# Attention step of a two-layer hybrid block: the scores' second part ahead of the transposes on TensorE, the scaling and the output copy ahead of the transposes' rounding on ScalarE

## The reference, cut to what matters

```
s = einsum('bqhgd,bkhd->bhgqk', q, k) * scale      # fp32 scores
p = softmax(s)                                     # swa: masked, with a sink
o = einsum('bhgqk,bkhd->bqhgd', p, v)
y = sigmoid(g_m)*((o_m*silu(z_m)) @ w_o_mla) + ... # also swa and ax
x = x + gate * (y @ w_out)
```

## Time and profile before

| what | value |
|---|---|
| median of 3 runs | 1756.91 us |
| the profiled execution's own time | 1756.88 us |
| its span | 1755.1 us |
| TensorE busy | 1679.7 us |
| ScalarE busy | 1049.0 us |
| VectorE busy | 1037.7 us |
| GpSimd busy | 625.0 us |
| mean granted TensorE clock | 0.987 of full speed |

### The profile page before, as it was taken

The page is one execution under the profiler, slowest core; times in us unless marked ns, Lnnn a source line. Parts: engine busy times, 40 slices in busy tenths (PEclk is TensorE's granted clock), DMA queues, the critical chain, the costliest instruction groups (busy, mean ns, idle before and its releaser), DMA issues.

```text
span 1755.1 us, 26992 instructions
## 1 busy us (share of the span) xinstructions
PE 1679.7 (96%) x10400; PEld 1471.6 (84%) x10400; DVE 1037.7 (59%) x2164; ACT 1049.0 (60%) x1919; POOL 625.0 (36%) x426
## 2 busy tenths in 40 slices
PE   7899999999999999999999999999999998999997
PEld 3778888889888899999889996788888887888787
DVE  6445766665566655545774556566676666555633
ACT  3435777776667767765221254678777678777322
POOL 2433333333333332323322344344344433333442
PEclk9999999999999999999999999999999999999999
DMA  9111111111121112012635222111122221212642
GB/s 332 40 37 29 26 46 37 49 31 49 49 55 49 42 31 55 26 48 57 219 117 197 90 87 61 41 38 46 51 53 67 72 73 32 69 52 53 204 148 93
DMA packets 178531, 129.51 MB, mean 74 GB/s; under 512 B 21658, under 2 KB 167652, under 8 KB 178404
## 3 DMA queue, kind: packets, MB, share of 16 engines
q1 hardware_dynamic: 174240, 115.36, 23.0%
q10 hardware_dynamic: 2884, 8.24, 1.3%
q0 software_dynamic: 1280, 4.20, 0.7%
HBM read 123.58 MB, written 4.19 MB: 73 GB/s over the span
## 4 chain that ended last, share of the span: by engine, by line
PE 77%; DVE 11%; ACT 8%; issue 3%; DMA 1%; POOL 1%; SPq 0%; DVEq 0%; ACTq 0%
PE acc L1393 56%; PE wide L1444 6%; PE ptp L1462 6%; PE pv L1475 4%; PE pv L1476 3%; DVE nmax L2051 2%; ACT e L1710 2%; DVE pt L2076 1%; ACT w_hi L1627 1%; DVE k_m L1579 1%; DVE q_s L1579 1%; ACT k_m L1570 1%; DVE k_s L1579 1%; DMA w_raw<-in_ada_w 1%; ACT e L1717 0%
## 5 line engine op out<-in xcount | busy, mean ns | idle before, releaser
L1834 POOL TENSOR_TENSOR w_lo<-w_raw,w_hi 128x1024 fp32r<-128x1024 f32 (+2 forms) x192 | 390.9, 2039 | 566.4 <-ACT w_hi L1627 565.0
L1393 PE MATMUL acc<-h_hi,w_hi 128*128 128x512 f32 (+2 forms) x1320 | 466.1, 354 | 13.0 <-DVE lf L1954 5.1
L1393 PE MATMUL acc<-h_hi,w_lo 128*128 128x512 f32 (+2 forms) x1320 | 462.4, 351 | 0.0
L1393 PE MATMUL acc<-h_lo,w_hi 128*128 128x512 f32 (+2 forms) x1320 | 458.6, 351 | 0.5 <-POOL h_lo L1896 0.5
L1393 PEld LDWEIGHTS acc<-h_hi,w_hi 128*128 128x128 f32 (+1 forms) x1320 | 249.5, 189 | 52.0 <-issue 12.4
L1725 ACT ACTIVATE pt<-ptp 128x512 fp32r<-128x512 f32 (+3 forms) x312 | 165.9, 563 | 198.2 <-PE ptp L1462 196.4
L1393 PEld LDWEIGHTS acc<-h_hi,w_lo 128*128 128x128 f32 (+1 forms) x1320 | 249.8, 189 | 34.0
L1393 PEld LDWEIGHTS acc<-h_lo,w_hi 128*128 128x128 f32 (+1 forms) x1320 | 246.9, 189 | 34.8 <-POOL h_lo L1896 0.9
L2051 DVE TENSOR_REDUCE nmax<-wide 128x1 f32<-128x768 f32 (+3 forms) x240 | 190.0, 792 | 112.1 <-PE wide L1444 108.6
L1888 POOL TENSOR_TENSOR o_t<-o_half,o_t 64x256 f32<-64x256 f32 x120 | 91.9, 766 | 436.9 <-DVE o_half L2083 434.8
L1717 ACT ACTIVATE e<-e,einv 128x768 f32<-128x768 f32 (+3 forms) x240 | 193.4, 806 | 57.2 <-DVE einv L2068 56.8
(11 more groups left out here) (215 smaller groups left out, 3065.8 us busy)
## 6 DMA issues: line engine op xcount, KB each, us to landing
w_raw<-in_w_in SPq DMA_DIRECT2D x102, 512.0 KB, 3.9
w_raw<-in_ada_w SPq DMA_DIRECT2D x48, 512.0 KB, 5.3
w_raw<-in_w_out SPq DMA_DIRECT2D x16, 512.0 KB, 3.5
w_raw<-in_w_in SPq DMA_DIRECT2D x16, 256.0 KB, 3.2
w_raw<-in_w_o_mla SPq DMA_DIRECT2D x16, 256.0 KB, 2.7
w_raw<-in_w_o_swa SPq DMA_DIRECT2D x16, 256.0 KB, 2.7
w_raw<-in_w_o_ax SPq DMA_DIRECT2D x16, 256.0 KB, 2.8
w_raw<-in_mla_w_uq SPq DMA_DIRECT2D x16, 144.0 KB, 2.3
```

Source lines behind the costliest of these rows:

```text
L1393: ins = nc.tensor.matmul(dst, lhs, rhs, start=first, stop=last)
L1834: nc.gpsimd.tensor_tensor(w_lo[s][:, 0:k], w_raw[s][:, 0:k], f(w_hi[s][:, 0:k]), ALU.subtract).then_inc(w_lo_ready, 1)
```

## The change

Inside each step of the loop, the transposes' event `T` moves from behind `PV` to behind `SB`, `N` and `OC`, and `OC` moves from behind `X` to ahead of `T`.

```diff
             valued, waiting = waiting[:2], waiting[2:]
-            for t in valued:
-                T(t)
             if u:
                 SB(u)
             if 0 < i <= len(units):
                 emit("N", u=units[i - 1])
+            if turned:
+                emit("OC", pa=turned)
+            for t in valued:
+                T(t)
             if u:
                 X(u)
-            if turned:
-                emit("OC", pa=turned)
             for t in valued:
                 emit("TL", t=t)
```

## The result

The changed kernel takes **1786.86 us** (median of 4 runs, 1786.74 to 1788.28) against 1755.95 us for the kernel before in the same session. The ratio is 1.0177, 95% interval 1.0165 to 1.0189: slower by 30.9 us. The forecast was 1775 us, range 1749 to 1791. The profiled execution has a span of 1785.1 us, 30.0 more than before.

A forecast was written before the change was run, and what follows sets the result against it. TensorE, busy 96% of the span, was taken as the bound. Terms 12.0 − 1.2 + 3.2 + 5.0 + 2 + 3 − 6 gave +18 us on 1756.88 us: 1775 us, range 1749 to 1791.

The forecast's parts named there:

- What bounds it: Whole kernel: TensorE, busy 96%; inside the attention its values' matmuls wait 31 times, scores 3 times, 32.3 us in all.
- The late step, +1.0 us: Step at 1244 us, reciprocal late: roundings follow scaling and copy, the chain ends 1.0 us later, all of it lost.
- The early step, −0.4 us: Step at 650 us, reciprocal early: scaling fills idle time, chain 0.4 us shorter, exponential 0.7 us earlier, worth nothing there.
- The values' waits: Values' matmuls: output's sum late +12.0, early −1.2; low part +3.2; new waits for steps not yet stalling +5.0 us.
- Lost cover at scores, +2: TensorE's scores lose the transposes' cover while waiting for the exponential: some four places at 0.5 us, +2 us.
- The clock, +3: TensorE's clock falls to 1.2 GHz behind long waits: two more such waits, about 1.5 us lost each, +3 us.
- Catching up, −6: A longer TensorE stall lets the other engines catch up, and earlier exponentials bring the reciprocal forward: −6 us.
- the bounds of the unknown terms: Cover (0 to +5), new waits (0 to +15) and catching up (−15 to 0) were said to span 1757 to 1794 us.
- Rival A: The shorter chain wins: most stalls of the values' matmuls have an early reciprocal and shrink, 1749 us; chance 0.20.
- The rule on the queues: ScalarE's and VectorE's queues are strictly first in, first out: a waiting scaling holds the roundings; otherwise near 1750 us.
- B: The two cancel: stalls grow at late steps, vanish at early ones, and projections absorb the rest, 1757 us; chance 0.15.
- C: The delay feeds itself: each late exponential makes the next reciprocal late, 56 steps at +0.7, 1796 us; chance 0.10.

The follow-up runs named there:

- run 1: Only TensorE's half of the change, scores ahead of transposes, ScalarE's order as before, against the kernel before: 1764.37 us, ratio 1.0050.
- runs 5 and 6: Scaling by a column of ones, without the wait for the reciprocal: 5 on the changed kernel, 1749.04 us; 6 on the kernel before, 1752.99 us.
- Run 9: The changed kernel with VectorE's reciprocal moved from the next step's start to its own step's end: 1742.41 us, ratio 0.9921 against the kernel before.
- ScalarE's half alone: Kernel before with only ScalarE's scaling and output copy moved ahead of the rounding, TensorE keeping transposes ahead of scores: 1795.79 us, ratio 1.0226.
- runs 8, 10 and 11: Against the kernel before: 8, scaling behind copy and exponential, 1821.44 us; 10 and 11, reciprocal and scaling at own step's end, scores or transposes first, 1809.55, 1819.19 us.

## Why the prediction was right, point by point

- **What bounds it.** Right in the main. The loss appears in the attention, as waits of the values' matmuls (+19.0 us), of scores (+2.3) and as clock (+10.0); the rest of the kernel did not get longer.
- **The late step, +1.0 us.** The chain measured 3.94 us against 2.92: +1.02. But "all of it is lost" did not hold: TensorE's step grew by 0.74 us. **The early step, −0.4 us**, and the exponential 0.7 earlier: measured −0.43 and 0.79.
- **The values' waits.** My terms for them (12.0 − 1.2 + 3.2 + 5.0) were +19.0 net, and the matmuls' rows grew by 19.0. That the two agree to the tenth is luck. The split was off: waits for the output's sum grew by 17.0, with 14 new ones, and for the low part by 2.0; I had 10.8 and 3.2, and 5 for new ones of either kind. The rows do not say how much an old wait grew by.
- **Lost cover at scores, +2.** Measured +2.3 at matmuls; without the late scaling it is larger, 8.2 us of waits in run 1.
- **The clock, +3: too small.** I had two more falls, and there were four more, one of ten microseconds: +10.0 us in the attention. The mean clock of the whole trace, 0.987 to 0.985, hides this, as outside the attention less clock was missing (−6.7 us).
- **Catching up, −6: too large.** The late step shows that it exists, 0.27 us there. But the attention's waits grew by the full 20.9 us, what the terms without it add up to (19.0 and 2), so nothing of it is left over in the total.
- **The size.** +18 was forecast and about +31 measured. By the terms, the missing parts are the clock (7), catching up (6) and some 3 to 4 us of waits that the matmuls' rows do not show; the time outside the attention, which was 4.9 us shorter in the profiled execution, takes from these. The measured time lies nearer to the upper end of the range than to 1775.
- **Two slips in the working.** "Six take 0.7 at 1244": the row of six holds three matmuls of 256 columns and three of 512, and they took 1.14 us. The 0.24 us for two was right all the same (670.75 to 670.99 in the changed kernel). And the bounds of the unknown terms give 1759 to 1794, not 1757.
- **A number I did not foresee.** Rival A was to decide at fewer than some 25 waits for the reciprocal. There are 165. I had counted only the 56 in which ScalarE came to the scaling ahead of the reciprocal in the order of before; with the scaling first it does so in 109 more. Most of these waits replace waits for transposes: the two together grew by only 18.6 us.
- **The rule on the queues.** That ScalarE keeps strict order (the Trainium skill, "TensorE: Matmul & The Clock Gate", section "Architectural detail: the array is 16× 32×32, not 1× 128×128") agrees with runs 5 and 6: taking away one wait of a later operand, with all work left in place, gave back 37.8 us.
- **The rivals.** A does not happen here. Run 9, with the reciprocal early, comes nearest to it: 48 waits for the reciprocal, 20.4 us of waits of the values' matmuls and not 31.2, and 1742.41 us. B did not come. C, the delay that feeds itself, did not come at 1796 either, but ScalarE's half alone reached 1795.8.

## What to carry to other kernels

Before an operation that waits for another engine's tiny result is put ahead of one whose operand is ready, look where the tiny result stands in *its* engine's queue, however much idle time there seems to be. Here the 0.16 us reciprocal behind up to 2.8 us of key splits decided between −0.8% and +1.8% for the same order on ScalarE. When a reordering loses, move the producer of the awaited value before the order is given up. And moving the waiting operation elsewhere is no cure by itself: behind the exponential (runs 8, 10 and 11) the same scaling cost 3 to 4%.

## What the runs showed of the hardware that was not expected

The clock fell behind single waits of TensorE of 1.6 to 3.0 us: behind six of fourteen waits of 1.5 us or more in the changed kernel's attention, and behind three of four before. So a reordering that added 21 us of waits added 10 us of clock to them.

Neither kind of row gives a stall of TensorE in full. Waits at matmuls with the clock came to 30.9 us and waits at weight loads with the clock to 38.5, where the attention grew by 34.9.

The mean clock of a whole trace does not tell what a change did. Outside the attention, where no order was changed, between 10.7 and 18.9 us of clock were not granted in the fourteen traces. Run 9 shows what this does to a comparison. Its span is 15.7 us shorter than before. Its attention is 1154.4 us long, 11.9 us shorter, of which 1.9 us are clock; the other 3.8 us lie outside the attention, where 12.0 us of clock were missing and not 17.9. So most of what run 9 gains in the attention is waits that are gone (34.1 to 26.4 us at matmuls), and part of its gain is not the change's.
